# More places for the experts' weights: single buffers in the expert stage, twenty-three weight places in a new order, and turned tiles moved between halves of gather or combine

## The reference, cut to what matters

```python
def moe(x, w_router, b_router, w1, w3, w2):
    e_idx, gates = route(xf, w_router, b_router)   # 2 of 16 experts for each token, with gates
    ...                                            # tokens gathered by expert
    def expert_block(args):
        xb, e = args
        hb = jax.nn.silu(xb @ w1[e]) * (xb @ w3[e])
        return hb @ w2[e]
    ...                                            # results weighted by gates, added back by token
```

## Time and profile before

| | value |
|---|---|
| median of three runs | 1877.72 us |
| profiled execution, its own time | 1881.71 us |
| its span, first to last instruction | 1880.5 us |
| TensorE busy | 1714.5 us, 91% |
| VectorE / ScalarE / GpSimd busy | 797.5 / 613.4 / 121.1 us |
| moved by DMA | 544.87 MB, mean 290 GB/s |
| mean granted clock of TensorE | 0.981 |
| first expert layer's products | 156 to 597 us |
| second expert layer's products | 737 to 1180 us |

### The profile page before, as it was taken

How to read it: one execution, slowest core, us unless ns; L and a number is a source line. 1 busy time by engine, 2 the same in 40 slices (tenths; PEclk the granted TensorE clock), 3 DMA queues, 4 the chain that set the end, 5 groups by cost and what they waited for, 6 DMA issues and landing times.

```text
span 1880.5 us, 23783 instructions
## 1 busy us (share of the span) xinstructions
PE 1714.5 (91%) x9910; PEld 1120.7 (60%) x9910; DVE 797.5 (42%) x1526; ACT 613.4 (33%) x1159; POOL 121.1 (6%) x141
## 2 busy tenths in 40 slices
PE   7978999998887988999999888699999999999998
PEld 7954343333332975333333332487899889779986
DVE  4952110110002774111101100566788766748885
ACT  4531010100001561100100000366566554746664
POOL 0000000000000000000000000033111000501110
PEclk9989999999999898999999999799999999999999
DMA  9348999999999638999999999443455544335550
GB/s 398 130 150 351 420 419 420 420 420 420 420 420 418 238 140 306 421 420 420 419 420 420 419 420 419 183 152 135 145 189 182 181 159 176 114 126 187 189 178 26
DMA packets 75361, 544.87 MB, mean 290 GB/s; under 512 B 8432, under 2 KB 8432, under 8 KB 9456
## 3 DMA queue, kind: packets, MB, share of 16 engines
q1 hardware_dynamic: 74304, 540.05, 72.3%
q10 hardware_dynamic: 944, 3.22, 0.4%
HBM read 542.19 MB, written 1.05 MB: 289 GB/s over the span
## 4 chain that ended last, share of the span: by engine, by line
PE 69%; DMA 18%; DVE 6%; ACT 4%; issue 1%; POOL 1%; SPq 0%; DVEq 0%; ACTq 0%
PE PS L898 23%; DMA ring<-in_w 17%; PE PS L335 12%; PE PS L337 12%; PE PS L336 12%; PE PS L910 2%; PE PS L875 2%; PE PS L649 1%; DVE wl L318 1%; ACT F L1024 1%; PE PS L963 1%; POOL sm L430 1%; DVE X L540 1%; DMA X<-in_x 1%; ACT wh L312 1%
## 5 line engine op out<-in xcount | busy, mean ns | idle before, releaser
L898 PE MATMUL PS<-ring,F 128*64 128x512 f32 x2304 | 515.7, 596 | 54.1 <-DMA ring<-in_w 33.7
L318 DVE TENSOR_TENSOR wl<-ring,wh 128x512 fp32r<-128x512 f32 x512 | 368.0, 738 | 191.6 <-ACT wh L312 188.7
L312 ACT ACTIVATE wh<-ring 128x512 fp32r<-128x512 f32 x512 | 319.7, 631 | 299.4 <-PE PS L337 295.8
L898 PEld LDWEIGHTS PS<-ring,F 128*64 128x64 f32 x2304 | 158.1, 137 | 392.4 <-issue 269.8
L335 PE MATMUL PS<-xh,wl 128*128 128x256 f32 x1216 | 352.0, 289 | 6.9 <-DVE xl L1555 2.1
L336 PE MATMUL PS<-xl,wh 128*128 128x256 f32 x1216 | 345.4, 284 | 0.0
L337 PE MATMUL PS<-xh,wh 128*128 128x256 f32 x1216 | 345.3, 284 | 0.0
L335 PEld LDWEIGHTS PS<-xh,wl 128*128 128x128 f32 x1216 | 234.6, 193 | 11.4 <-issue 5.8
L336 PEld LDWEIGHTS PS<-xl,wh 128*128 128x128 f32 x1216 | 234.7, 193 | 0.6
L337 PEld LDWEIGHTS PS<-xh,wh 128*128 128x128 f32 x1216 | 234.5, 193 | 0.0
L335 PE MATMUL PS<-wh,xl 128*128 128x512 f32 x368 | 150.2, 408 | 12.1 <-DVE wl L318 5.0
(11 more groups left out here) (332 smaller groups left out, 1713.2 us busy)
## 6 DMA issues: line engine op xcount, KB each, us to landing
ring<-in_w SPq DMA_DIRECT2D x288, 1024.0 KB, 26.1
early<-in_w SPq DMA_DIRECT2D x48, 1024.0 KB, 21.9
ring<-in_ffn_up SPq DMA_DIRECT2D x44, 1024.0 KB, 4.9
F<-in_w SPq DMA_DIRECT2D x24, 1024.0 KB, 21.8
ring<-in_ffn_down SPq DMA_DIRECT2D x22, 1024.0 KB, 4.8
Z<-in_w SPq DMA_DIRECT2D x12, 1024.0 KB, 23.1
XT<-in_w SPq DMA_DIRECT2D x12, 1024.0 KB, 23.8
ring<-in_even_w_in SPq DMA_DIRECT2D x10, 1024.0 KB, 17.9
```

The lines of the kernel that those rows point to most:

```text
L312: act.e.activation(self.wh[:, p % NPIECE, :], self.piece_source(p), ACT.Copy).then_inc(*self.up("w_hi", p))
L318: dve.e.tensor_tensor(self.wl[:, p % NPIECE, :], self.piece_source(p), f32(self.wh[:, p % NPIECE, :]), ALU.subtract).then_inc(*self.up("w_ ...
L898: t = pe.e.matmul(PS[64 * half:64 * half + 64, bank, :], lhs(k), weights[:, a:a + 512], start=(k == 0), stop=(k == 7))
```

## The change

It does four things.

1. **One copy of each intermediate.** S, Gs, Gt, xg and hT exist once; `th`, `sl` and `hh` become one tile `hh`, written in place. The expert stage's part of F shrinks from 8192 to 4352 columns. The three tables of the forget gate move into the end of F, which grows from 13568 to 14720 columns; `decay` is zeroed by GpSimd after the last expert of layer 1. The even mixer's views move down in F.
2. **Twenty-three places.** F now holds five chunks (places 12 to 16), `early` four (17 to 20), Z one, XT one.
3. **A new order of the first 23 chunks**, `FIRST_SLOTS`. In layer 0: two places of F that need no wait, 8 of the ring, three of F, 4 of the ring, `early`, Z, XT. In layer 1: 8 of the ring, five of F, 4 of the ring, `early`, Z, XT. The waiting places of F wait for `g_lo(mixer, 3)`, the last split of the mixer's gated output (VectorE, L420), instead of the mixer's last piece.
4. **A new order on TensorE.** The hidden tile is turned into bank 4 between the two halves of combine or gather, the gates after the second half of combine, and w2's product goes to bank 5.

```diff
-RING, SMALL_RING, EXTRA = 12, 7, 8
+RING, SMALL_RING, EXTRA = 12, 7, 11
...
+F_SLOTS, SPLIT_SLOTS, Z_SLOT, XT_SLOT = range(12, 17), range(17, 21), 21, 22
+FIRST_SLOTS = ([12, 13] + [None] * 8 + [14, 15, 16] + [None] * 4 + [17, 18, 19, 20, 21, 22],
+               [None] * 8 + [12, 13, 14, 15, 16] + [None] * 4 + [17, 18, 19, 20, 21, 22])
...
-        self.F = sb("F", [128, 13568])
+        self.F = sb("F", [128, 14720])
...
-        mixed = self.at("w_used", PIECES["ow_out" if layer else "ew_out"] + 15)
-        if i >= RING + EXTRA or (layer, i) == (0, RING):
+        slot, mixer, norm = SLOT[n], ("ow_out" if layer else "ew_out"), ("ln2" if layer else "ln0")
+        if n - CHUNK[f"moe{layer}"] >= RING + EXTRA:
             return []
-        if i < RING + 6:
-            return [mixed]
-        return [self.at("turned", "ln2" if layer else "ln0", 3) if i == RING + 6 else self.at("tokens_turned", layer, 3)]
+        if slot in F_SLOTS:
+            return [] if layer == 0 and slot < 14 else [self.at("g_lo", mixer, 3)]
+        if slot in SPLIT_SLOTS:
+            return [self.at("w_used", PIECES[mixer] + 15)]
+        return [self.at("turned", norm, 3) if slot == Z_SLOT else self.at("tokens_turned", layer, 3)]
...
+        if q == 0:
+            ...
+        else:
+            pe.wait_ge(at("xg1", layer, q - 1) if half else at("gates_t", layer, q - 1))
...
+            pe.wait_ge(at("xg0", layer, q), at("hid_t", layer, ex - 1) if ex else at("ranks_read", layer))
+            self.tensor_product(layer, ex, 0, 4, slots, (lambda: self.tensor_gather(layer, 0, 1)) if ex == 0 else None)
+            pe.wait_ge(*((at("y0", layer, ex - 1), at("y1", layer, ex - 1)) if ex else (at("counts_read", layer),)))
             self.tensor_product(layer, ex, 1, 5, slots)
             if o == 0:
                 if q:
-                    self.tensor_combine(layer, q - 1)
-                pe.wait_ge(at("gate_slots", layer, q), at("hid_t", layer, ex - 1) if ex else at("xg0", layer, 0))
...
-                pe.wait_ge(at("gates_t", layer, q))
-            elif q < 7:
-                self.tensor_gather(layer, q + 1)
-                pe.wait_ge(at("xg0", layer, q + 1))
+                    self.tensor_combine(layer, q - 1, 0)
+                self.tensor_turn_hidden(layer, ex)
+                if q:
+                    self.tensor_combine(layer, q - 1, 1)
+                self.tensor_turn_gates(layer, q)
             else:
-                pe.wait_ge(at("hid_t", layer, ex - 1))
-            pe.wait_ge(at("hidden", layer, ex))
...
+                if q < 7:
+                    self.tensor_gather(layer, q + 1, 0)
+                self.tensor_turn_hidden(layer, ex)
+                if q < 7:
+                    self.tensor_gather(layer, q + 1, 1)
             pe.wait_ge(at("hid_t", layer, ex))
-            self.tensor_product(layer, ex, 2, 7, lambda k: hT[:, k % 4 * 128 + k // 4 * 64:k % 4 * 128 + k // 4 * 64 + 64])
+            self.tensor_product(layer, ex, 2, 5,
+                                lambda k: v["hT"][:, k % 4 * 128 + k // 4 * 64:k % 4 * 128 + k // 4 * 64 + 64])
...
+            if o and q < 7:
+                self.vector_gate_slots(layer, q + 1)
             dve.wait_ge(self.expert_done(layer, ex, 1), at("silu", layer, ex))
...
             if o == 0 and q < 7:
                 self.vector_pick(layer, q + 1)
-                self.vector_gate_slots(layer, q + 1)
...
     def forget_pool(self):
+        pool.wait_ge(self.expert_done(1, 15, 2))
+        e.memset(f32(self.decay[:, :]), 0.0).then_inc(*up("fg_zero"))
```

More of the change, by code:

```diff
@@ L116, in _place_stream @@
         slots = list(range(RING if n < CHUNK["aq0"] else SMALL_RING))
-        i = -1
+        slot = None
         if kind == "expert":
[L119 to L123, removed]
+            layer = int(n >= CHUNK["moe1"])
+            i = n - CHUNK[f"moe{layer}"]
+            if i < RING + EXTRA:
+                slot = FIRST_SLOTS[layer][i]
+            elif i < 128:
                 slots += range(RING, RING + EXTRA)
+        if slot is None:
             slot = min(slots, key=lambda x: -1 if last[x] is None else last[x])
@@ L219, in __init__ @@
                             for n, i in (("qh", 10), ("ql", 11))]}
[L220 to L223, removed]
+        self.decay, self.wfh, self.wfl = (nc.alloc_sbuf_tensor_at(n, [128, 384], F32R, offset=f_at + 4 * (13568 + 384 * i))
+                                          for i, n in enumerate(("decay", "wfh", "wfl")))
         self.pick = sb("pick", [128, 16], F32R)
@@ L226, in __init__ @@
         self.it = sb("it", [128, 8], I32)
-        self.slots = [self.ring[:, i, :] for i in range(RING)] + [self.F[:, 11520:13568], self.F[:, 9472:11520]] + [
-            self.early[:, i, :] for i in range(4)] + [self.Z[:, :, :].rearrange("p h d -> p (h d)"),
-                                                      self.XT[:, :, :].rearrange("p k t -> p (k t)")]
+        assert nc.sbuf_base <= split_at
+        self.slots = [self.ring[:, i, :] for i in range(RING)] + [
+            self.F[:, 12672 - 2048 * i:14720 - 2048 * i] for i in range(5)] + [self.early[:, i, :] for i in range(4)] + [
+            self.Z[:, :, :].rearrange("p h d -> p (h d)"), self.XT[:, :, :].rearrange("p k t -> p (k t)")]
         self.over = [dma_sem(f"s_over_{n}") for n in ("pe", "act", "dve", "w")]
@@ L294, in sync_load @@
         for n in range(first, min(last, len(KIND))):
-            if SLOT[n] >= RING:
+            if KIND[n] == "expert" and SLOT[n] >= RING:
                 sp.wait_ge(*self.extra_free(n))
@@ L626, in even_views @@
             sg=self.fv(4300, 4), acc=self.fv(5400, 4), bc=self.fv(6500, 4), bacc=self.fv(7600, 4),
-            sq=self.fv(8700, 4), rs=F[:, 9800:10056], dgs=[F[:, 10056 + i * 128:10184 + i * 128] for i in range(6)],
+            sq=self.fv(4300, 4), rs=F[:, 8700:8956], dgs=[F[:, 8956 + i * 128:9084 + i * 128] for i in range(6)],
             b2=self.sm[:, 8:12], gh=self.sm[:, 0:4], bh=self.sm[:, 4:8],
@@ L842, in moe_views @@
         return dict(
[L843 to L849, removed]
+            S=F[:, 0:256].rearrange("p (h n) -> p h n", h=2), Gs=F[:, 256:768].rearrange("p (i h n) -> p i h n", i=2, h=2),
+            Gt=F[:, 768:1280].rearrange("p (h s t) -> p h s t", h=2, s=2),
+            xg=F[:, 1280:2304].rearrange("p (k s) -> p k s", k=8), hh=F[:, 2304:2816], hT=F[:, 2816:3328],
+            Y=[F[:, 3328 + i * 512:3840 + i * 512] for i in range(2)])
     def sv(self, a, n=16):
@@ L856, in expert_done, with tensor_gather @@
         return self.at("expert_chunk", CHUNK[f"moe{layer}"] + 12 * ex + 4 * w + 3)
-    def tensor_gather(self, layer, q, halves=(0, 1)):
+    def tensor_gather(self, layer, q, half):
         pe, at, v = self.pe, self.at, self.moe_views()
[L861 to L877, removed]
+        pe.wait_ge(at("picked", layer, q))
+        if q == 0:
+            pe.wait_ge(self.normed_bank_free(layer, 2 + half))
+            for b in range(4):
+                pe.wait_ge(at("x_tokens", layer, b))
+        else:
+            pe.wait_ge(at("xg1", layer, q - 1) if half else at("gates_t", layer, q - 1))
+        for k4 in range(4):
+            k = 4 * half + k4
+            for h in range(2):
+                t = pe.e.matmul(self.PS[:, 6 + half, k4 * 128:k4 * 128 + 128], self.X[:, h, k * 128:k * 128 + 128],
+                                v["S"][:, h, :], start=(h == 0), stop=(h == 1))
+        t.then_inc(*self.up("gathered", layer, q, half))
     def normed_bank_free(self, layer, q):
@@ L900, in tensor_product, with tensor_combine, tensor_turn_hidden, tensor_turn_gates @@
             t.then_inc(*self.up("expert_chunk", n))
-    def tensor_combine(self, layer, q):
+    def tensor_combine(self, layer, q, h):
         pe, v = self.pe, self.moe_views()
         pe.wait_ge(self.at("gates_t", layer, q), self.at("y0", layer, 2 * q + 1), self.at("y1", layer, 2 * q + 1))
-        for h in range(2):
[L906 to L911, removed]
+        for d in range(2):
+            b = 2 * h + d
+            if q == 0:
+                pe.wait_ge(self.at("x_tokens", layer, b))
+            t = pe.e.matmul(self.PS[:, b, :], v["Gt"][:, h, d, :], v["Y"][d], start=(q == 0), stop=(q == 7))
+            t.then_inc(*self.up("combined", layer, q, b))
+    def tensor_turn_hidden(self, layer, ex):
+        pe, hh = self.pe, self.moe_views()["hh"]
+        pe.wait_ge(self.at("hidden", layer, ex))
+        for j in range(4):
+            t = pe.e.transpose(self.PS[:, 4, j * 128:j * 128 + 128], hh[:, j * 128:j * 128 + 128], self.ident[:, :])
+        t.then_inc(*self.up("hid_turned", layer, ex))
+    def tensor_turn_gates(self, layer, q):
+        pe, Gs = self.pe, self.moe_views()["Gs"]
+        pe.wait_ge(self.at("gate_slots", layer, q), self.at("xg0", layer, q))
+        for h in range(2):
+            for s in range(2):
+                a = (2 * h + s) * 128
+                t = pe.e.transpose(self.PS[:, 6, a:a + 128], Gs[:, s, h, :], self.ident[:, :])
```

(9 more changed lines are left out.)

76 lines of the change are left out of this document (22 added, 54 removed).

## The result

The changed kernel takes 1866.26 us (median of 5 runs, 1860.77 to 1868.88) against 1880.24 us for the kernel before (median of 5 runs, 1876.89 to 1883.62). The ratio is 0.9919, 95% interval 0.9894 to 0.9944, so the change makes the kernel 0.8% faster, about 15 us. The profiled execution took 1861.7 us, span 1860.4.

What follows compares the result with a forecast made beforehand. Weights were the bound: an expert layer ends with its 192nd chunk, set by the chunks landed before the first release. Gains of 7.5 us in each layer, 15.0 together, took 1877.72 to 1862.7 us; range 1857 to 1872.

Steps and rivals of the forecast that it cites:

- The bound: Expert layers end when their 192nd chunk has landed, set by how many chunks have landed at the first release.
- the room of 22 and 26 us: How much sooner TensorE would end layer 0 and layer 1 if weights were there.
- Layer 0, -7.5: Before layer 0's first release 23 chunks are in instead of 20: -7.5 us, ends 0 and -7.5.
- R to L: SyncE's first issue needing a used chunk (R, forecast near 158 and 731 us) to TensorE's start on the last chunk.
- Layer 1, -7.5: Places in layer 1 come in time before its first release, with 0.5 us to spare: -7.5 us, poor end -4.
- Rival A: Layer 1 gains nothing because its five F places come too late: 1870.2 us; chance 0.12 with what lies between.
- TensorE's order, 0: A pair of experts falls by 3 x 0.69 to 50.6 us, worth 0 while weights are the bound.
- Where TensorE first waits: In layer 0 TensorE runs out of weights near 390 us instead of 407.2.
- Zeroing, 0: GpSimd's 0.42 us of zeroing moves to the end of layer 1, hidden in a 3.94 us wait: 0.
- B: Transfers after the first release also run at full rate, 2.5 us more in each layer: 1857.7 us; chance 0.07.
- C: Transfers were hidden anyway, or the bound passes to TensorE at once: 1877.7 us; chance 0.06.
- D: TensorE starves more often behind 390 us, its clock falls: 1974 us if all 158 chunks fall; chance 0.03 with other stalls.

Runs made afterwards that it cites:

- halved kernels: Expert chunks behind the first filling of the places fetched only by half: kernel before 1835.55 us (0.9756), changed kernel 1797.67 us (0.9553).
- the repetition: The changed kernel measured again, unaltered, on another chip against the kernel before: 1866.73 us, ratio 0.9926.
- late F: Changed kernel, but F's waiting places wait for the mixer's last piece instead of the last split of its output: 1879.17 us, 0.9988 to the kernel before.
- serial order: Changed kernel with its 23 places, but TensorE does the side job whole and only then turns the hidden tile: 1863.35 us, 0.9902 to the kernel before.
- 20 places: Changed kernel with three of F's five places unused, TensorE's new order kept: 1882.09 us, 1.0005 to the kernel before.

## Why the prediction was right

- **The bound.** The layers do end with their 192nd chunk. (The row of GB/s reads "100 to 300" outside the plateaus only in the main: its first slice is 398, those ahead of the plateaus are 351 and 306, the last is 26. Nothing hung on it.) The halved kernels show it from the other side: with the weights taken away as the bound, the kernel before falls by 46 us, from 1881.38 to 1835.55; 1830 had come out of the room of 22 and 26 us.
- **Layer 0, -7.5.** Measured -8.2 from R to L in the first pair of traces. The issues came where they were expected (F at 121.93 for 122.2, R at 158.27). In the single microseconds from 154 to 159 the DMA engines move 401, 320, 41, 8 and 0 GB/s, which makes 1.8 us of work at 420, so the 23rd chunk was in near 156, as worked out (155.8). Why the gain is 0.7 us above three transfers is not shown.
- **Layer 1, -7.5.** Measured -7.1. That there is nothing to spare was right in that execution: its second mixer was short, F came 36.2 us ahead of R instead of 38.0, and transfers ran through without a pause. In the repetition F came 39.7 us ahead, and the queue ran dry just before R at 735.35: 360 GB/s from 732 to 735, 41 from 735 to 736. Both times R to L is 432 us. (R was forecast for 731 and the last chunk for 1163; the first trace has 726.01 and 1158.54, mostly by the mixer's 4.3 us.) So one sentence of the forecast was too strict, that beyond the 0.5 us to spare each us by which the queue runs late is a us lost: by it the first execution would have lost 1.3 us, and late F, some 13 us late, lost 9.9, with the transfers behind R at 420 GB/s. Rival A, the loss of this layer's gain, did not come; late F shows that its mechanism is real.
- **TensorE's order, 0.** Right, by serial order and by 20 places. The size beside it was somewhat too small: 2.42 us a pair instead of 3 x 0.69 = 2.07. A copy with what stands around it is 0.67 in the chain (519.78 + 0.45 to 520.90), so the three are 2.0. The rest is in the transposes, of which four take 0.67 us when TensorE has waited for a copy ahead of them and 0.44 in a row, and in the products, which take 20.75 instead of 20.82.
- **Where TensorE first waits.** I put it at 407 before and at 390 after. In layer 0 TensorE's first wait for a chunk ends at 425.57 us before and at 394.25 after. I had read the start of a transfer in the chain as the start of the wait; the chain's entry begins at the issue, and its 28.30 us run to the landing. TensorE itself waits no more than 0.6 us for a chunk there. The shift was to be 17 us and is 31. That 390 lies so near to 394 is partly luck: a start that was too early met a saving of a pair that was too small. Nothing of the sum hung on it, since both lie well ahead of the layer's end.
- **Zeroing, 0.** It stands in a gap of GpSimd, after which it still waits for VectorE for 3.57 us:

```profile
1173.57 0.41 POOL L1928 MEMSET decay<- 128x384 f32 x1
1177.56 0.55 POOL L437 TENSOR_TENSOR sm<-sm,mhalf 128x1 f32<-128x1 f32 x1 [3.57 <-DVE sm L433]
```

- **The other rivals.** B (the low rates behind R go too) is wrong for the changed kernel: 350 GB/s against 344. Its condition, a backlog at R, was met in the kernel with late F and there the rate is 420. C is refuted by the places. D, the clock, did not come: 1.00 at 500 to 560 us, though TensorE waits for weights from 394 on. Its waits are some 0.55 us behind 1.94 us of products. In the loop that the Trainium skill describes (page "TensorE: Matmul & The Clock Gate", section "HAM oscillation — how this bites in real kernels") the wait for a tile is longer than the products of the tile, so this trace says nothing against that page. The 358 GB/s of the Trainium skill (page "DMA: Bandwidth & Descriptors", section "Specifications") are given there as a stack's 716 divided between two cores. This kernel runs on one core; the plateaus of its traces are at 420, and R to L shrank by 2.4 to 2.9 us a place.
- **The level.** 1862.7 was forecast, 1866.26 measured. Two more runs of the kernel before moved its median from 1877.72 to 1880.24, which is 2.5 of the 3.6; the size of the step, 15.0, agrees with the ratio's 15.2 and with the 14.0 between the medians.

## What to carry to other kernels

When a stage ends with the last of a fixed number of transfers at full rate, its end is set by how many have landed when the first one has to wait for a consumed buffer. Count the idle time of the DMA engines before that moment: a buffer was worth about one transfer time here (2.4 to 2.9 us for 2.5) when it came free early enough to be filled in it. When the buffer comes free counts as much as that it exists, since in a queue that issues in order it holds back what stands behind it: F 12 to 14 us later left 2 of the 15 us. A reordering on the compute engine can be worth much and show nothing as long as weights are the bound; take half of the bytes away to see it.

## What the runs showed that I had not expected

- One and the same kernel has a second mixer of 138.88 and of 144.89 us, at a mean granted clock of 0.93 and 0.88, while VectorE and ScalarE work equally long. The whole step of the change is only two and a half times as large as that difference. A single pair of traces would have shown 20.1 us (1880.5 to 1860.4) where the ratio gives 15.
- In the kernel with late F eleven runs lie between 1878.48 and 1879.88 us, closer together than those of any other version (the changed kernel's five lie within 8.1 us). Its transfers run without a pause from the mixer's last piece on, so that what happens between this and the first release does not count. That this is the cause is argued, not shown.
- The rate behind the first release depends on the backlog of the queue: 420 GB/s over 14 us with one, and some 340 without. The 350, 344 and 307 GB/s of the changed kernel, the kernel before and the one with 20 places can hardly be ranked. In all three the queue had run dry, and with 20 places R is 1.2 us later, so that a part of the idle time falls into the stretch. Over 14 us from where the first released transfer moves bytes (159.5 us, and 160.7 with 20 places) the rates are 338, 333 and 321.
